# Keys and the retention's gate by seven products, head norms block by block, convolution taps moved behind

## The chip, the cores and the metric

One NeuronCore of a Trainium2 chip runs one two-layer block in fp32: a mixing stage, 32 routed experts, a second mixing stage, 16 routed experts. The metric is device microseconds of one execution, the median of several runs. Lower is better.

## The reference, cut to what matters

The change lies wholly in the first layer's mixing stage. There 256 latent tokens and 256 context tokens, each of 1024 numbers, go through the columns of one projection:

```python
u_ctx = h_ctx * (1 + csc) + csh
kv = u_ctx @ w_in[:, K_OFF:G_OFF] + b_in[K_OFF:G_OFF]
s_f = final_state(k_c, v_c, lg_f); s_b = final_state(k_c[:, ::-1], v_c[:, ::-1], lg_b)
u_lat = h_lat * (1 + sc) + sh
q, k, v, g, glu, gates = split(u_lat @ w_in + b_in)
q, k = rope(q), rope(k)
o = retention_bidir(q, k, v, lg_f, lg_b, s_f, s_b)       # 8 heads, keys of 128, values of 256
ret = silu(g) * head_norm(o)                             # 2048 columns
y_a = ret @ w_ret_out
z = za * sigmoid(zb)                                     # from glu
z = silu(layernorm(depthwise_conv(z, 31 taps))) 
y_b = z @ w_conv_out + b_conv_out
mix = (sigmoid(ga) * y_a + sigmoid(gb) * y_b) @ w_mix_out + b_mix_out
```

Keys (1024 columns) and values (2048) are wanted for latent and context tokens; queries, the gate g (2048), glu and gates for latent tokens alone.

## The kernel before

All engines run one hand-written order; they meet at semaphores. SyncE (SP) loads weights in blocks of 2 MB (1024 x 512 numbers) into eight bays of SBUF; in the mixing stage three of them (`ring`) take turns. `make_jobs` (line 84 on) lists the jobs and gives each load its bay, from `EARLY_BAYS` and then from `ROUNDS["mix1"]`; `load` (L404) issues a load when the last job that read its bay is done. So the place of a job in TensorE's order says when a later load can start.

TensorE's order in this stage: the modulation, glu, keys, queries, values, the heads, the gate g, the gates, then the output of the retention and of the convolution, and the mixing projection. A job of kind `cm8` is 32 matmuls of 128 x 128 by 256 columns (L835); a job of the gate g, kind `tm8`, is 16 matmuls of 512 columns (L846). The two key blocks have a job for latent (`cm8`) and one for context tokens (`cm8c`). The profile shows each fp32 matmul as two records.

The four value blocks are computed for latent and context tokens together by seven products instead of eight (Strassen's scheme over halves of the contraction and halves of the columns): `seven_products` (L942, matmuls at L957) multiplies sums of tokens (`u_sums`, made at L1453) by quarters of the weights or their sums (`add_weights`, L1455 to L1462). Each product is eight matmuls of 256 columns in one of four PSUM buffers `MB`. VectorE adds every product to the places it belongs to (`add_product`, L1482; two halves for products 0 to 4, one for 5 and 6; L1493, L1494, L1497), makes the next block's weight sums, and puts two taps of the convolution behind each product (`convolve`, L1400; taps at L1406 and L1408).

The convolution has 248 taps on VectorE, 8 channel tiles of 31. They are spread as filling over the stage: 64 during glu, 64 during the keys, 56 during the values, 16 in the heads, 48 during the gate g. Behind the last one comes the sum over channels (L1413), for which TensorE's `mean_of_sums` (L1026) waits after the last gates job.

The heads. TensorE per head h (L962 to L990): scores of head h+1 (two matmuls against the context keys, two against the latent ones), one of eight modulation jobs (L823), the output of head h. VectorE per head: the latent and the context scores times their decays (L1524, L1526), the argument of the decays of head h+2 (`decay`, L1475, L1476), statistics of head h-1 (L1513, L1516), the sum of two context decays of head h+2 (`context_decay`, L1481), two taps. ScalarE: copy of the output of head h-1 (L612), exponential of the decays of head h+2 (L596), four exponentials of the context decays (L606). The ties between them:

```python
pe.wait_ge(pc_sb, h)            # scores(h): VectorE's product with the context scores of head h-1
act.wait_ge(dec_arg, h + 1)     # decays(h): VectorE's decay(h)
act.wait_ge(pc_sb, h - 1)       # context_decays(h)
dve.wait_ge(eq_ready, h + 1)    # context_decay(h): ScalarE's exponentials
```

After the heads VectorE takes a copy of the last modulation, TensorE turns it (`turn_late`), VectorE folds it with gains and biases (`late_modulation`, L1355), normalises all 16 head tiles (L1548), and then per block of g adds the bias (L1440), waits for ScalarE's silu (L637) and multiplies (L1554). TensorE transposes the result (`turn_ret`, L1001) one block later.

Of the kernel before, what the change touches and what calls it, by code (L numbers as in the profile page):

```python
# [26 lines left out]
ALU = mybir.AluOpType  # L27
# [3 lines left out]
P = 128  # L31
D = 1024
L = 256
DT = D // P
# [41 lines left out]
ROUNDS = {"mix1": (2, 0, 1), "moe0": (4, 2, 3, 6, 5, 0, 1, 7), "mix2": (0, 1, 2, 4), "moe1": (7, 0, 3, 6, 1, 2, 4, 5)}  # L76
# [3 lines left out]
EARLY_BAYS = (0, 1, 0, 1, 2, 4, 5, 3, 0, 1, 2, 0, 1, 2, 1, 2, 1)  # L80
SUM_BAY = 0
# [5 lines left out]
def make_jobs():  # L87
# [11 lines left out]
    def experts(n):  # L99
        for e in range(EXPERTS[n] - 2):  # L100
            for q in range(3):
# [3 lines left out]
    order = (("mix1", (("ada", 4, ["ada"]), ("piece", PIECES, []), ("glu", 4, ["cm8"]), ("k", 2, ["cm8", "cm8c"]),  # L105
# [28 lines left out]
def build(nc, a):  # L134
# [3 lines left out]
    with ExitStack() as ctx:  # L138
# [105 lines left out]
        w_sums = [ring[:, SUM_BAY, D * i:D * (i + 1)].rearrange("p (a n) -> p a n", a=4) for i in range(4)] + [raw]  # L244
        retT, gT, mT, SQ = Vc, V, kT, qT
# [119 lines left out]
        def seven_wait(eng, b, p):  # L365

            if p == 6:
                eng.wait_ge(job_done, J["v", b, 0]["i"] + 1)
            else:
                eng.wait_ge(seventh, 6 * b + p + 1)  # L370

        def quarters(b):

            W = bays[loads[J["v", b, 0]["w"]]["bay"]].rearrange("p (k n) -> p k n", n=512)
            return W[:, 0:4, 0:256], W[:, 0:4, 256:512], W[:, 4:8, 0:256], W[:, 4:8, 256:512]
        lat1, lat2, ctx1, ctx2 = uT[:, 0:4, :], uT[:, 4:8, :], ucT[:, 0:4, :], ucT[:, 4:8, :]
# [122 lines left out]
        def _(pool):  # L499
# [5 lines left out]
            for n in range(8):  # L505

                if n >= 6:
# [29 lines left out]
        def _(act):  # L537
# [49 lines left out]
            for r, (src, b, bias) in enumerate((("k", 0, "b_k"), ("k", 1, "b_k"), ("q", 0, "b_q"), ("q", 1, "b_q"))):  # L587
                raw_copy(r, src, b, bias)
# [45 lines left out]
            for b in range(4):  # L634
                j = J["g", b, 0]
# [176 lines left out]
        def _(pe):  # L812
# [122 lines left out]
            for b in range(2):  # L935
                job(J["k", b, 0])
                pe.wait_ge(u_ready, PIECES + 1)
                job(J["k", b, 1])
# [1180 lines left out]
```

## Time and profile before

| | |
|---|---|
| median of 3 runs | 1500.07 us (1499.38 to 1500.78) |
| the profiled execution | 1499.55 us |
| its span | 1497.7 us |
| TensorE busy, over the span | 97% |
| VectorE, ScalarE busy | 36%, 15% |
| HBM read | 431.61 MB, 290 GB/s over the span |

The span is cut into instructions; a group names line, engine, operation and the tiles written and read. Idle time in front of a group is put down to what released it. A row of the timeline shows a run of like instructions: start, length, count. TensorE's rows overlap by the end of a matmul, some 0.16 us, so durations are best read from one start to the next. Of the mixing stage, TensorE spends 81 to 136 us on the keys, 136 to 164 on the queries, to 267 on the values, to 327 on the heads, to 385 on the gate g and to 441 on the gates.

### The profile page before, as it was taken

The numbers are of one execution on the slowest core, as the hardware profiler recorded it, in microseconds if no ns is written. First come the engines' busy times: TensorE is split into PE (matmuls) and PEld (weight loads), VectorE is DVE, ScalarE is ACT, GpSimd is POOL, SyncE is SP. The second block draws the span as 40 slices with busy tenths as digits, with TensorE's granted clock in tenths as the row PEclk, the third lists the DMA queues.
The fourth block names the chain that finished last, engine by engine and source line by source line (L and its number), as shares of the span: only waits on it lengthen the run. The fifth ranks groups of instructions, "written<-read, shape, count | busy, mean of one in ns | idle before, by whom it ended". The sixth has DMA issues, their size and how long they took to land.

```text
span 1497.7 us, 19676 instructions
## 1 busy us (share of the span) xinstructions
PE 1446.1 (97%) x8450; PEld 973.3 (65%) x8450; DVE 541.3 (36%) x1127; ACT 227.7 (15%) x438; POOL 17.8 (1%) x38
## 2 busy tenths in 40 slices
PE   8999899999999999999999998999999999999996
PEld 6888788664788887555544444445788886455542
DVE  0467898665402145222222111114223242211122
ACT  0210200321121004110111101012121022111011
POOL 0000000000000010000000000000010000000000
PEclk9999999999999999999999999999999999999999
DMA  9722132864343577999999999997564747999986
GB/s 382 294 97 93 57 113 78 310 258 162 133 168 131 225 313 278 369 426 427 428 426 426 427 429 427 427 417 314 151 223 156 286 169 303 429 428 427 427 339 257
DMA packets 36330, 435.43 MB, mean 291 GB/s; under 512 B 4353, under 2 KB 5769, under 8 KB 10009
## 3 DMA queue, kind: packets, MB, share of 16 engines
q1 hardware_dynamic: 33408, 427.89, 70.1%
q0 software_dynamic: 1664, 4.52, 1.0%
q10 hardware_dynamic: 1176, 1.84, 0.8%
q8 instruction: 64, 1.05, 0.3%
q14 instruction: 18, 0.14, 0.0%
HBM read 431.61 MB, written 2.62 MB: 290 GB/s over the span
## 4 chain that ended last, share of the span: by engine, by line
PE 80%; DMA 15%; DVE 4%; issue 0%; ACT 0%; SPq 0%; POOL 0%; DVEq 0%; POOLq 0%; ACTq 0%
PE PP L835 22%; PE PP L1146 17%; PE PP L1161 9%; PE MB L957 6%; PE MB L1130 5%; PE PP L846 5%; DMA ZC<-in_w_moe 5%; PE PP L873 3%; DMA RA<-in_w_moe 2%; DMA ring<-in_w_moe 2%; DMA Vc<-in_w_moe 2%; DMA uT<-in_w_moe 2%; PE PP L905 2%; PE PP L1122 1%; DMA ring<-in_w_ada 1%; DVE ZC L1408 1%
## 5 line engine op out<-in xcount | busy, mean ns | idle before, releaser
L835 PE MATMUL PP<-uT,ring 128*128 128x256 f32 x832 | 181.2, 379 | 0.0
L835 PEld LDWEIGHTS PP<-uT,ring 128*128 128x128 f32 x832 | 157.7, 190 | 21.8 <-issue 0.5
L1408 DVE SCALAR_TENSOR_TENSOR ZC<-ZC,vec 128x256 f32<-128x256 f32 x240 | 116.3, 484 | 7.9
L1815 DVE TENSOR_SCALAR V<-V 128x1 f32<-128x1 f32 x50 | 7.7, 154 | 307.2 <-PE PP L1146 307.2
L1146 PE MATMUL PP<-ring,const 128*64 128x256 f32 x992 | 112.1, 380 | 5.1 <-DMA ring<-in_w_moe 4.5
L1130 PE MATMUL MB<-V 64*128 64x512 f32 x400 | 112.4, 640 | 1.7 <-DVE V L1838 0.9
L1146 PEld LDWEIGHTS PP<-ring,const 128*64 128x64 f32 x992 | 72.2, 137 | 49.1 <-issue 11.6
L1830 DVE SCALAR_TENSOR_TENSOR V<-V 128x256 f32<-128x256 f32 x100 | 48.5, 485 | 108.7 <-PE MB L1130 94.0
L699 ACT ACTIVATE V<-PP 128x256 f32<-128x256 f32 x50 | 19.2, 385 | 380.1 <-PE PP L1146 380.1
L1161 PE MATMUL PP<-ring,const 128*64 128x512 f32 x336 | 76.7, 599 | 0.0
L846 PE MATMUL PP<-ring,uT 128*128 128x512 f32 x160 | 69.5, 593 | 0.0
L1146 PE MATMUL PP<-ZC,const 128*64 128x256 f32 x512 | 58.3, 380 | 7.7 <-DMA ZC<-in_w_moe 7.7
L1146 PE MATMUL PP<-RA,const 128*64 128x256 f32 x512 | 58.3, 380 | 3.9 <-DMA RA<-in_w_moe 3.7
L703 ACT ACTIVATE const<-small 128x512 f32 x50 | 31.8, 636 | 166.2 <-PE PP L1146 165.8
L1146 PEld LDWEIGHTS PP<-ZC,const 128*64 128x64 f32 x512 | 36.7, 137 | 30.1 <-DMA ZC<-in_w_moe 8.3
L835 PE MATMUL PP<-Vc,ring 128*128 128x256 f32 x256 | 55.6, 379 | 0.0
L1146 PEld LDWEIGHTS PP<-RA,const 128*64 128x64 f32 x512 | 36.6, 137 | 28.3 <-DMA RA<-in_w_moe 8.2
L846 PEld LDWEIGHTS PP<-ring,uT 128*128 128x128 f32 x160 | 30.1, 190 | 37.0 <-issue 37.0
L835 PEld LDWEIGHTS PP<-Vc,ring 128*128 128x128 f32 x256 | 48.6, 190 | 6.6
L1161 PEld LDWEIGHTS PP<-ring,const 128*64 128x64 f32 x336 | 22.3, 136 | 46.8 <-issue 45.1
L1836 DVE TENSOR_TENSOR V<-PP,uT 128x512 f32<-128x512 f32 x32 | 22.1, 692 | 80.4 <-PE PP L1161 80.4
L1130 PEld LDWEIGHTS MB<-V 64*128 64x128 f32 x400 | 30.3, 184 | 30.4 <-issue 30.2
(433 smaller groups left out, 1880.0 us busy)
## 6 DMA issues: line engine op xcount, KB each, us to landing
ring<-in_w_moe SPq DMA_DIRECT2D x54, 2048.0 KB, 18.9
RA<-in_w_moe SPq DMA_DIRECT2D x22, 2048.0 KB, 16.3
ZC<-in_w_moe SPq DMA_DIRECT2D x22, 2048.0 KB, 17.8
KQ<-in_w_moe SPq DMA_DIRECT2D x18, 2048.0 KB, 19.0
Vc<-in_w_moe SPq DMA_DIRECT2D x17, 2048.0 KB, 18.9
extra<-in_w_moe SPq DMA_DIRECT2D x17, 1792.0 KB, 16.5
ring<-in_w_ada SPq DMA_DIRECT2D x12, 2048.0 KB, 9.0
ring<-in_w_gates SPq DMA_DIRECT2D x7, 2048.0 KB, 8.0
```

What stands on the lines that cost most here:

```text
L703: nc.scalar.activation(xs, xsc[:, :, bass.ds(at, SLOTS)], ACT.Copy).then_inc(m["xs_ready"], 1)
L835: ins = pe.matmul(out[:, c, :], W[:, k * width + at:k * width + at + P], X[:, k, :], start=k == 0, stop=k == K - 1)
L846: ins = pe.matmul(out[:, 2 * t:2 * t + 2, :].rearrange("p a n -> p (a n)"), X[:, k, t * P:(t + 1) * P], W[:, k * 512:(k + 1) * 512], start ...
L873: ins = pe.matmul(out[:, c, :], W[:, k * 512 + c * P:k * 512 + (c + 1) * P], X[:, k, :], start=k == 0 and c % 2 == 0, stop=k == DT - 1 and ...
L905: ins = pe.matmul(glu_at(b, c), W[:, at:at + P], uT[:, k, :], start=k == 0 and c % 2 == 0, stop=k == DT - 1 and c % 2 == 1)
L957: ins = pe.matmul(MB[n % 4][:, t, :], x[:, k, t * P:(t + 1) * P], y[:, k, :], start=k == 0, stop=k == 3)
L1130: ins = pe.matmul(acc[t][g], S[rows, t * P:(t + 1) * P], ys[rows, :], start=first, stop=done == "acc_done", tile_position=(SLOTS * g, 0))
L1146: ins = pe.matmul(bank[q][SLOTS * g:SLOTS * (g + 1), 0:L], x[:, k, :], weights(W, k * 512 + g * 256, 256), start=k == 0, stop=k == DT - 1, ...
L1161: ins = pe.matmul(bank[2][SLOTS * g:SLOTS * (g + 1), :], hts[:, c % 2, SLOTS * (c // 2):SLOTS * (c // 2 + 1)], weights(W, c * D + g * 512, ...
L1408: ins = V_.scalar_tensor_tensor(conv[:, t, :], zpad[:, t, k:k + L], tap, conv[:, t, :], ALU.mult, ALU.add)
L1830: linked(V_.scalar_tensor_tensor(Sk[:, c], placer[:, c], slotcol, weightr[:, c], ALU.is_equal, ALU.mult), k, c + 2)
L1836: ins = V_.tensor_tensor(ys, bank[2], gate_row, ALU.mult)
```

## The change

- The keys get the seven products too. The order becomes queries, then six blocks of seven products (two of keys, four of values). For keys the weight sums stand as the stationary operand, so that the result has channels on partitions. Their weight sums go to the tiles of the values (`k_sums`). The rotations of queries come first; those of keys work in place once a block is complete.
- The gate g, wanted for latent tokens alone, gets seven products over halves of the latent's tokens, of the contraction and of the columns. A product there is four matmuls of 256 columns. VectorE makes five sums of half tokens (in head 1), five weight sums per block (those of the first block in heads 5, 6 and 7), adds every product to quarters of the block and works the bias in.
- The head norms are made for one block at a time, inside the gate blocks. The gate product of a block stands two products into the next one.
- Taps: 8 instead of 16 at each glu block, none beside the keys as such, 1, 1, 2, 2, 2, 4 behind a product in the six blocks (none where a rotation stands), 6 instead of 2 per head, and the 88 that are left after the last gate block. The folds of the modulation come behind them.
- Bays are renamed: the sums of weights use bay 2 instead of 0.

The diff, cut to its core:

```diff
-EARLY_BAYS = (0, 1, 0, 1, 2, 4, 5, 3, 0, 1, 2, 0, 1, 2, 1, 2, 1)
-SUM_BAY = 0
+EARLY_BAYS = (0, 1, 0, 1, 2, 4, 5, 3, 0, 1, 2, 0, 1, 0, 1, 0, 1)
+SUM_BAY = 2
...
-    order = (("mix1", (("ada", 4, ["ada"]), ("piece", PIECES, []), ("glu", 4, ["cm8"]), ("k", 2, ["cm8", "cm8c"]),
-                       ("q", 2, ["cm8"]), ("v", 4, ["seven"]), ("ada", 8, ["ada"]), ("g", 4, ["tm8"]), ("gates", 4, ["cm8"]),
+    order = (("mix1", (("ada", 4, ["ada"]), ("piece", PIECES, []), ("glu", 4, ["cm8"]), ("q", 2, ["cm8"]),
+                       ("k", 2, ["seven"]), ("v", 4, ["seven"]), ("ada", 8, ["ada"]), ("g", 4, ["seven"]), ("gates", 4, ["cm8"]),
...
-                    dense += (src != "ada" or b == 11) and (src, b) != ("glu", 2) and src != "v"
+                    dense += (src != "ada" or b == 11) and (src, b) != ("glu", 2) and src not in ("k", "v", "g")
...
+        k_sums = [home[:, 4 * i:4 * i + 4, :] for home in (V, Vc) for i in range(4)]
...
+        SEVEN = [("k", b) for b in range(2)] + [("v", b) for b in range(4)] + [("g", b) for b in range(4)]
+        G7 = 6
+        gate_raw = [small[:, i, :].rearrange("p (a n) -> p a n", a=LT) for i in range(2)]
+        halves = [[uT[:, 4 * k:4 * k + 4, P * t:P * (t + 1)] for k in range(2)] for t in range(LT)]
+        tok_sums = [extra[:, 512 * q:512 * (q + 1)].rearrange("p (a n) -> p a n", a=4) for q in range(5)]
+        of_half = lambda t, half: flat(t)[:, half * 2048:half * 2048 + 1024].rearrange("p (a n) -> p a n", a=4)
+        of_rest = lambda t, half: flat(t)[:, half * 2048 + 1024:(half + 1) * 2048].rearrange("p (a n) -> p a n", a=4)
+        g_sums = [[kw, of_half(V, 0), of_half(V, 1), Kc[:, 0:4, :], Kc[:, 4:8, :]],
+                  [of_rest(V, 0), of_rest(V, 1), KQ[:, 0:4, :], KQ[:, 4:8, :], KQ[:, 8:12, :]]]
...
+        def sum_at(i, q):
+
+            if i >= G7:
+                return g_sums[(i - G7) % 2][q]
+            return w_sums[q] if i >= 2 else k_sums[(5 * i + q) % 8]
+
+        def gate_bank(n):
+
+            x = J["gates", 0, 0]["pair"]
+            return PP[x if n % 4 < 2 else 1 - x][:, 2 * (n % 2), :]
         lat1, lat2, ctx1, ctx2 = uT[:, 0:4, :], uT[:, 4:8, :], ucT[:, 0:4, :], ucT[:, 4:8, :]
...
-                    j = J["g", n - 6, 0]
-                    pool.wait_ge(pair_free[j["pair"]], j["use"] + 1)
-                elif n >= 2:
-                    pool.wait_ge(seven_kept, 7 * (n - 1))
+                if n >= 2:
+                    pool.wait_ge(seven_kept, 7 * (n + 1))
...
+            for b in range(2):
+                act.wait_ge(seven_kept, 7 * (b + 1))
+                act.wait_ge(rope_done, 2 + b)
+                keys = kT[:, 4 * b:4 * b + 4, :]
+                nc.scalar.activation(swapped[0:64], keys[64:128], ACT.Copy)
...
+            for i in range(G7):
+                seven_products(i)
+
+            def gate_products(b):
+
+                i = G7 + b
+                B11, _, _, B22 = quarters(i)
+                made = 5 * G7 + 10 + 5 * b
+                for p, (x, y, sums) in enumerate(((tok_sums[0], B11, 5 * G7 + 6), (tok_sums[1], B22, 5 * G7 + 7),
+                                                  (halves[0][0], sum_at(i, 0), made + 1), (halves[1][1], sum_at(i, 1), made + 2),
+                                                  (tok_sums[2], sum_at(i, 2), made + 3), (tok_sums[3], sum_at(i, 3), made + 4),
+                                                  (tok_sums[4], sum_at(i, 4), made + 5))):
+                    n = 7 * i + p
+                    if p == 0:
+                        w_wait(pe, seven_job(i)["w"])
+                    pe.wait_ge(sums_made, sums)
+                    if n >= 7 * G7 + 4:
+                        pe.wait_ge(seven_kept, n - 3)
+                    elif n % 2 == 0:
+                        j = J["gates", p // 2, 0]
+                        pe.wait_ge(pair_free[j["pair"]], j["use"])
+                    for k in range(4):
+                        ins = pe.matmul(gate_bank(7 * b + p), x[:, k, :], y[:, k, :], start=k == 0, stop=k == 3)
+                    ins.then_inc(job_done if p == 6 else seventh, 1)
...
-                    j = J["k", 1, 1]
-                    pe.wait_ge(pair_free[j["pair"]], j["use"] + 1)
-                    pe.wait_ge(seven_kept, 26)
+                    pe.wait_ge(seven_kept, 40)
...
-                job(J["g", b, 0])
+                gate_products(b)
                 if b:
                     turn_ret(b - 1)
+            pe.wait_ge(seven_kept, 7 * len(SEVEN) - 2)
             job(J["gates", 0, 0])
             turn_ret(3)
+            pe.wait_ge(seven_kept, 7 * len(SEVEN))
             for b in range(1, 4):
...
+            def late_folds():
+
...
-                convolve(b * A_JOB, (b + 1) * A_JOB)
+                convolve(8 * b, 8 * (b + 1))
...
+            def add_weights(i, q):
+
+                if q == 0:
+                    w_wait(dve, seven_job(i)["w"])
+                if i == 1 and q >= 3:
+                    dve.wait_ge(seventh, q)
+                B11, B12, B21, B22 = quarters(i)
                 x, y, op = ((B12, B22, ALU.subtract), (B21, B11, ALU.subtract), (B11, B22, ALU.add), (B11, B12, ALU.add),
-                            (B21, B22, ALU.add))[i]
-                V_.tensor_tensor(w_sums[i], x, y, op).then_inc(sums_made, 1)
-            job_wait(dve, J["q", 0, 0])
-            for i in range(4):
-                add_weights(0, i)
-            rope(2)
-            rope(3)
-            add_weights(0, 4)
...
+            def taps(n):
+                tap_at[0] += n
+                convolve(tap_at[0] - n, tap_at[0])
+            tap_at = [step]
+            for i in range(G7):
                 for p in range(7):
-                    add_product(b, p)
-                    if p > 1 and b < 3:
-                        add_weights(b + 1, p - 2)
-                    convolve(step, step + 2)
-                    step += 2
-                if b < 2:
+                    add_product(i, p)
+                    if p > 1 and i + 1 < G7:
+                        add_weights(i + 1, p - 2)
+                    if (i, p) in ((0, 3), (1, 3), (2, 3)):
+                        rope(i + 1)
+                    else:
+                        taps((1, 1, 2, 2, 2, 4)[i])
+                if i in (2, 3):
...
-                convolve(step, step + 2)
-                step += 2
+                if h == 1:
+                    (a11, a12), (a21, a22) = halves
+                    for out, x, y, op in zip(tok_sums, (a21, a11, a11, a21, a12), (a22, a12, a22, a11, a22),
+                                             (ALU.add, ALU.add, ALU.add, ALU.subtract, ALU.subtract)):
+                        V_.tensor_tensor(out, x, y, op).then_inc(sums_made, 1)
+                if h == 5:
+                    add_weights(G7, 0)
+                elif h == 6:
+                    add_weights(G7, 1)
+                    add_weights(G7, 2)
+                elif h == 7:
+                    add_weights(G7, 3)
+                    add_weights(G7, 4)
+                taps(6)
...
+            def normalise(b):
+
+                for h in (2 * b, 2 * b + 1):
+                    for t in range(LT):
+                        o = On[:, t, h * DV:(h + 1) * DV]
+                        ins = V_.tensor_scalar(o, o, mv[:, t, h, 0:1], rstd[:, t * HEADS + h:t * HEADS + h + 1], ALU.subtract, ALU.mult)
+                link(ins)
+
+            def gate_ret(b):
+
                 dve.wait_ge(g_silu, b + 1)
                 o = On[:, :, b * 512:(b + 1) * 512]
-                say(dve, V_.tensor_tensor(o, o, raw2, ALU.mult), ret_ready, b + 1)
-                convolve(step + 12 * b, step + 12 * (b + 1))
...
+                one, two = ([out[:, t, 256 * half:256 * (half + 1)] for half in range(2)] for t in range(LT))
+                bias = [biasr[:, b % 2, 256 * half:256 * (half + 1)] for half in range(2)]
+                if p < 2:
+                    dve.wait_ge(bias_full[b % 2], 16 * ((4 + b) // 2 + 1))
+                    plus, minus = ((two[0], bias[0]), (two[1], bias[1])) if p == 0 else ((one[1], bias[1]), (one[0], bias[0]))
+                    V_.tensor_tensor(plus[0], M, plus[1], ALU.add)
+                    ins = V_.scalar_tensor_tensor(minus[0], M, -1.0, minus[1], ALU.mult, ALU.add)
+                else:
+                    for out in ((one[1], two[1]), (two[0], one[0]), (one[0], two[1]), (two[1],), (one[0],))[p - 2]:
+                        ins = V_.tensor_tensor(out, out, M, ALU.add)
+                say(dve, ins, seven_kept, n + 1)
+            for b in range(4):
+                for p in range(7):
+                    add_gate_product(b, p)
+                    if p == 1 and b:
+                        gate_ret(b - 1)
+                    if p > 1 and b < 3:
+                        add_weights(G7 + b + 1, p - 2)
+                    if p == 3:
+                        normalise(b)
+            gate_ret(3)
+            taps(DT * TAPS - tap_at[0])
+            late_folds()
 
```

## Rows read from the trace of the kernel before

**Rows 1.** Page, chain that ended last: share of the span by engine

```profile
PE 80%; DMA 15%; DVE 4%; issue 0%; ACT 0%; SPq 0%; POOL 0%; DVEq 0%; POOLq 0%; ACTq 0%
```

**Rows 2.** Chain in order of time, experts' stage: start us, us, what

```profile
836.53 34.22 DMA Vc<-in_w_moe
```

**Rows 3.** Timeline of TensorE, values: start us, us, engine, line, out<-in, records

```profile
108.67 13.98 PE L835 MATMUL PP<-uT,ring 128*128 128x256 f32 x64
...
163.93 7.07 PE L957 MATMUL MB<-ring,small 128*128 128x256 f32 x32
...
182.06 8.83 PE L957 MATMUL MB<-ring,extra 128*128 128x256 f32 x32 [4.16 <-DVE Vc L1494]
190.73 3.62 PE L957 MATMUL MB<-small,extra 128*128 128x256 f32 x16
...
266.70 1.03 PE L974 MATMUL MB<-KQ,Kc 128*128 128x256 f32 x4
```

**Rows 4.** Windows: us, busy of PE, PEld, DVE, ACT, POOL; PEclk, DMA share, GB/s

```profile
184.00:186.00 2.00, 2.00 (x6) 1.60 (x5) 1.89 (x5) 0.00 (x0) 0.00 (x0) 0.50 0.03 8
...
268.00:270.00 2.00, 0.59 (x3) 0.19 (x1) 1.93 (x5) 0.00 (x0) 0.49 (x1) 1.00 0.68 197
```

**Rows 5.** Timeline of TensorE, one head

```profile
284.71 1.03 PE L974 MATMUL MB<-KQ,Kc 128*128 128x256 f32 x4
...
286.53 1.92 PE L823 MATMUL PP<-ring,sT 128*32 128x512 f32 x16
...
291.94 1.03 PE L974 MATMUL MB<-KQ,Kc 128*128 128x256 f32 x4
```

**Rows 6.** Timeline of VectorE, the same head

```profile
282.89 0.69 DVE L1524 SCALAR_TENSOR_TENSOR small<-MB,small 128x512 f32<-128x512 f32 x1
...
284.09 0.74 DVE L1475 SCALAR_TENSOR_TENSOR small<-const,lgs 128x512 f32<-128x512 f32 x1
...
285.66 0.75 DVE L1513 BATCH_NORM_STATS2 bst<-RA 128x6 f32<-128x256 f32 x2
286.45 0.25 DVE L1516 BATCH_NORM_AGGREGATE mv<-bst 128x2 f32<-128x6 f32 x2
288.36 0.69 DVE L1481 TENSOR_TENSOR small<-small 128x512 f32<-128x512 f32 x1 [1.66 <-ACT small L606]
288.97 1.00 DVE L1408 SCALAR_TENSOR_TENSOR ZC<-ZC,vec 128x256 f32<-128x256 f32 x2
290.00 0.69 DVE L1524 SCALAR_TENSOR_TENSOR small<-MB,small 128x512 f32<-128x512 f32 x1
```

**Rows 7.** Timeline of ScalarE, the same head

```profile
285.66 0.63 ACT L596 ACTIVATE small<-small 128x512 f32<-128x512 f32 x1 [0.15 <-DVE small L1476]
286.19 2.06 ACT L606 ACTIVATE small<-const,wctx,lgs 128x256 f32<-128x256 f32 x4
```

**Rows 8.** Groups of VectorE by form: xcount, busy us, mean ns, idle before

```profile
L1462 DVE TENSOR_TENSOR ring<-ring 128x1024 f32<-128x1024 f32 x16 | 19.3, 1224 | 0.4
...
L1817 DVE TENSOR_TENSOR const<-PP,V 128x256 f32<-128x256 f32 x50 | 21.3, 426 | 2.3
```

**Rows 9.** SP's issue of the gate weights; DMA issues with median us to landing

```profile
310.21 13.07 SPq L415 DMA_DIRECT2D ring<-in_w_g  x3
...
ring<-in_w_g SPq DMA_DIRECT2D x4, 2048.0 KB, 8.2
```

**Rows 10.** Timeline of TensorE, the gate g: first job, first turn, first gates job

```profile
327.18 27.71 PE L846 MATMUL PP<-ring,uT 128*128 128x512 f32 x64
354.73 1.04 PE L1007 MATMUL MB<-const,RA 128*128 128x128 f32 x8
...
384.82 13.98 PE L835 MATMUL PP<-uT,ring 128*128 128x256 f32 x64
```

**Rows 11.** Timeline of VectorE, end of the convolution

```profile
394.14 3.68 DVE L1413 TENSOR_REDUCE rs<-ZC 128x256 f32<-128x2048 f32 x1
441.66 2.35 DVE L1562 TENSOR_TENSOR ZC<-ZC,MB 128x1024 f32<-128x1024 f32 x2 [43.84 <-PE MB L1029]
```

More of the change, by code:

```diff
@@ L586, in raw_copy @@
                 nc.scalar.activation(swapped[64:128], raw[0:64], ACT.Copy).then_inc(sig_ready, 1)
-            for r, (src, b, bias) in enumerate((("k", 0, "b_k"), ("k", 1, "b_k"), ("q", 0, "b_q"), ("q", 1, "b_q"))):
-                raw_copy(r, src, b, bias)
+            for b in range(2):
+                raw_copy(b, "q", b, "b_q")
+            for b in range(2):
+                act.wait_ge(seven_kept, 7 * (b + 1))
+                act.wait_ge(rope_done, 2 + b)
+                keys = kT[:, 4 * b:4 * b + 4, :]
+                nc.scalar.activation(swapped[0:64], keys[64:128], ACT.Copy)
+                nc.scalar.activation(swapped[64:128], keys[0:64], ACT.Copy).then_inc(sig_ready, 1)
             nfb = cst("nfb", 512)
@@ L933, in _, with seven_products @@
             pe.wait_ge(ld_rest, 32)
[L935 to L938, printed above, removed]
             job(J["q", 0, 0])
             job(J["q", 1, 0])
[L942 to L949 removed]
+            pe.wait_ge(u_ready, PIECES + 1)
+            def seven_products(i):
+                B11, _, _, B22 = quarters(i)
+                made = len(u_sums) + 5 * i
+                for p, (x, q, y, sums) in enumerate(((u_sums[0], None, B11, 1), (u_sums[1], None, B22, 2), (lat1, 0, None, made + 1),
+                                                     (ctx2, 1, None, made + 2), (u_sums[2], 2, None, made + 3),
+                                                     (u_sums[3], 3, None, made + 4), (u_sums[4], 4, None, made + 5))):
+                    n = 7 * i + p
                     if p == 0:
[L951 removed]
+                        w_wait(pe, seven_job(i)["w"])
                     pe.wait_ge(sums_made, sums)
@@ L1481, in context_decay, with add_product @@
                 V_.tensor_tensor(Eqd[:, q:q + 2, :], Eqd[:, q:q + 2, :], Eqb[:, q:q + 2, :], ALU.add)
-            def add_product(b, p):
-                n = 7 * b + p
-                seven_wait(dve, b, p)
-                M = MB[n % 4][:, :, :]
-                at = lambda i: slice(512 * b + 256 * i, 512 * b + 256 * (i + 1))
-                lat, ctx = [Vt[:, :, at(i)] for i in range(2)], [Vct[:, :, at(i)] for i in range(2)]
-                bias = [biasr[:, b % 2, 256 * i:256 * (i + 1)].unsqueeze(1).to_broadcast([P, LT, 256]) for i in range(2)]
+            def add_product(i, p):
+                n, (src, b) = 7 * i + p, SEVEN[i]
+                seven_wait(dve, i, p)
+                M = MB[(n + 2) % 4][:, :, :]
+                if src == "k":
+                    at = lambda half: slice(4 * b + 2 * half, 4 * b + 2 * half + 2)
+                    lat, ctx = [kT[:, at(half), :] for half in range(2)], [Kc[:, at(half), :] for half in range(2)]
+                    bias = [vec[:, VCOLS["b_k"] + 4 * b + 2 * half:VCOLS["b_k"] + 4 * b + 2 * half + 2].unsqueeze(2).to_broadcast([P, LT, L])
+                            for half in range(2)]
+                else:
+                    at = lambda half: slice(512 * b + 256 * half, 512 * b + 256 * (half + 1))
+                    lat, ctx = [Vt[:, :, at(half)] for half in range(2)], [Vct[:, :, at(half)] for half in range(2)]
+                    bias = [biasr[:, b % 2, 256 * half:256 * (half + 1)].unsqueeze(1).to_broadcast([P, LT, 256]) for half in range(2)]
                 if p < 2:
-                    dve.wait_ge(bias_full[b % 2], 16 * (b // 2 + 1))
+                    if src == "v":
+                        dve.wait_ge(bias_full[b % 2], 16 * (b // 2 + 1))
                     plus, minus = ((ctx[0], bias[0]), (ctx[1], bias[1])) if p == 0 else ((lat[1], bias[1]), (lat[0], bias[0]))
```

82 lines of the change are left out of this document (36 added, 46 removed).

## The prediction, made blind

> **What bounds the kernel now.** I read the page's chain of waits first [rows 1]: TensorE carries 80% of the chain that ended last, DMA 15%, VectorE 4%. Then the chain in order of time. Its DMA pieces lie in the experts' stage, where landings of 2 MB succeed each other [rows 2]; those loads are released by TensorE's jobs of the mixing stage, so whatever moves the end of the gate jobs moves them, and everything behind, by the same amount. The question is therefore only when TensorE finishes the last gate job and the mean of the convolution behind it.
>
> TensorE's timeline from the keys to the heads [rows 3] gives the unit of the sum. Each program matmul of 256 columns stands as two records; a job of 32 of them takes 13.98 us with its last end, 13.82 to the start of the next, so one costs 0.432 us, and a product of eight 3.455 us. The 28 products of the values would take 96.7 us; they take 266.70 - 163.93 = 102.8. The missing 6.0 us are one place: TensorE waits 4.16 us for VectorE ahead of 182.06, and the next 32 records take 8.67 us (182.06 to 190.73) in place of 6.91, 1.76 us more. The windows say why [rows 4]: at 184 to 186 us the granted clock was 0.50, the 1.2 GHz level, after a pause of 4.2 us. At 268 to 270 us, with TensorE idle for 1.58 us, it stayed at 1.00.
>
> The third reading decides. In the retention's head loop TensorE's period is 7.23 us (284.71 to 291.94, [rows 5]) and looks like the bound. But VectorE's period is 7.11 us (282.89 to 290.00, [rows 6]), and no wait in it is on TensorE: its one wait, 1.66 us, is for ScalarE's exponentials. These start when VectorE's own decay operations end: exponential of the decays at 285.66, four of the context at 286.19, done at 288.25 [rows 7], and VectorE goes on at 288.36. So VectorE's loop is a closed chain of its own work and ScalarE's, 0.12 us from setting the pace, and TensorE's scores of the next head wait for VectorE's second product of this one.
>
> **The change, part by part.**
>
> *Keys, and the stall of the values.* Two blocks of 64 matmuls (lat and ctx) become two of 56: 16 x 0.432 = -6.9 us. The sums of tokens and of the first weights now come while the two query jobs run, and the first two blocks carry one tap per product. VectorE per block: five updates of two halves at 1.32 us (0.61 + 0.71 from one start to the next, where one takes 0.69 busy), two of one at 0.72, five weight sums at 1.14 (1.22 busy [rows 8], 0.08 overlapped) = 13.8 us; with six taps and a rotation (three operations of 1024, 3.8 us) 20.7 us, against 24.2 us of TensorE. The third block has twelve taps, a rotation and two decays, 26.9 us, but enters with some 7 us of lead and 3 free product buffers. No block stalls TensorE, and the 6.0 us go too. The next weights land in time: a bay frees at a block's end and three products, 10.4 us, pass before VectorE asks for it, against a landing of 8.2 us [rows 9]. Sum: -12.9 us; heads start at 253.8 instead of 266.7. ScalarE's two swaps of key halves are released by the block's last update and are asked for three products later: nothing.
>
> *Head loop, taps.* Two taps per head become six. The wait for ScalarE doesn't shrink: it hangs on the decays, which stand ahead of it, while the taps stand behind it. A tap costs 0.52 (two in 1.03, 288.97 to 290.00, [rows 6]), so the period becomes 7.11 + 4 x 0.52 = 9.2 us, above TensorE's 7.23. VectorE now sets the pace, and TensorE pauses 2.0 us before each scores.
>
> *Head loop, sums of half tokens.* In head 1 five additions of 512 elements, five times 0.61 = 3.05 us, in the same chain: +3.05.
>
> *Head loop, weights of the first gate block.* In head 5 VectorE waits for that block's weights. Its bay is freed by the modulation job of head 5; before, the load was issued at 310.21, the moment that job ended, and took 8.2 us [rows 9]. The job ends 3.8 us after the second product of head 5 (0.15 to TensorE, 1.8 scores, 1.9 job, [rows 5]); with issue and landing the weights are there 12.2 us after it. VectorE reaches the wait after decays 1.57, statistics 1.06, the wait of 1.7 and the addition 0.6, 4.9 us. It stands 7.3 us, with the taps and the products of heads 6 and 7 queued behind it, and TensorE's scores of head 7 wait for those. Then five weight sums: 1.14 here, 2.28 in each of heads 6 and 7. Before, nothing of VectorE waited for these weights.
>
> *The stage laid end to end.* Last product 253.8; VectorE's last update and four taps behind it, first two score products: 258.1. Six periods of 9.2 (heads 0 to 5), 55.3; sums of tokens 3.05; head 5's wait and sum 8.5: second product of head 6 at 324.9. Head 6 without decays: 1.06 + 2.28 + 3.12 + 1.2 = 7.7: 332.6. Head 7: 0.7 wait for the copied output, 1.06, 2.28, 3.12: 339.8. The copy of the modulation, 512 elements, takes 0.7 and TensorE's four small products some 0.85: gate products start at 341.4. The stage takes 87.7 us where it took 327.18 - 266.70 = 60.5: +27.2 us.
>
> *Clock.* TensorE's pause in heads 5 and 6 is 10.5 us, longer than the one that cost 1.76 us. I take 1.75 once: the output of head 6 is on the path there, as its statistics hold VectorE. In head 2 (5.0 us pause) a loss of that size hides in the next pause of 2.0. Bounds 0 (hidden) and 3.5 (another in head 7).
>
> *Gate products.* 4 x 28 matmuls of 0.432 = 48.4 and three turns of 0.88 (1.04 with its overlap) give 51.0; before, 384.82 - 327.18 = 57.6 [rows 10]: -6.6 us. VectorE needs per block five updates of two quarters (0.81) and two of one (0.46), from the nearest row of that form, 0.426 busy [rows 8]; five weight sums 5.7; four head norms at 0.35, the start-to-start of that form, 1.4; one gate product 1.26: 13.3 us against 12.97. Four buffers carry this 0.3 us; if an update of two takes 0.96, the low end of the lead is lost and it costs 1.7. I take 0. ScalarE's silu of 1.1 us starts at a block's end and is asked for two products, 3.5 us, later. POOL's bias loads are released one block ahead of use, as before.
>
> *Behind.* 88 taps are left for after the last gate: 45.7 and the reduction 3.7 [rows 11], 49.4 us. TensorE has 56.1 us of gate jobs. VectorE ends 4.5 us ahead, the folds of 1.7 us (nine operations of under 0.25) fit as well; before it idled 43.8 us there, until the mean released it at 441.66. Cost 0, and this cover is nearly gone: VectorE is what would be late next.
>
> *Sum.* -12.9 + 27.2 + 1.75 - 6.6 = +9.4 us on the profiled execution's 1499.55 us (span 1497.7), 0.5 us under the median of 1500.07: **1509.0 us**.
>
> **Rules of the skill.** The Trainium skill ("TensorE: Matmul & The Clock Gate", "A second HAM failure mode: psum-queue depth-cycling") says that short idles between groups of matmuls, if frequent, make the clock swing between its levels. This would speak against a head loop with a pause of 2 us in every 9.2. The short pause of rows 4 does not show it; by the rule the time would be the last rival's.
>
> **Rivals.**
> *The stretched loop hides (faster).* If the six taps fitted into the 1.66 us wait and the gate weights were there, the head stage would keep its 60.5 us, and only -12.9 and -6.6 would remain: 1480. It decides at TensorE's waits ahead of scores: none means this. Against it: the order of operations [rows 6, 7] puts taps behind the wait, and the load cannot be issued before head 5's job. Chance 0.08.
> *Pace only.* If the wait for the gate weights were absent (an earlier landing), the weight sums alone would remain and the stage be 5 to 6 us shorter: 1503 without clock loss. For it: only that one load's timing; against: the 310.21 issue. Chance 0.10.
> *VectorE late behind (slower still).* If updates of quarters run at the high bound, the gate stage grows by 1.7 and the tail eats the 4.5 us: 1511 to 1514. Chance 0.10.
> *Clock down through the heads.* At 1.2 GHz throughout, a head is 14.5 us and sets the pace: 8 x 14.5 = 116 us in place of 89.4: 1535. Chance 0.04.
> *The change does less than it says.* The edits replace every key and gate matmul, so the 32 fewer program matmuls are certain; no chance is set on it.
>
> **How the numbers follow.** The forecast holds 0.68. About 0.2%, 3 us, is what a measurement of this kernel can tell from no change. Range 1503 to 1513: its low end is pace only, its high end the clock's high bound with the quarter updates'; the two far rivals (0.12) and some of the third stay outside. Faster 0.09; same 0.06, out of pace only with a gain elsewhere; slower 0.85.
>
> **What would show it.** Right: TensorE's values without a wait; scores 9.2 us apart for most heads, each released by VectorE's second product; one wait of VectorE of about 7 us on the load of the gate weights in head 5; scores of head 7 some 10 us late; gate stage 51 us; the mean of the sums about 448 to 451 us and the first expert loads later by the same. Wrong: a head period still at 7.2, no VectorE wait on that load, or a wait of TensorE for the sum of the convolution.

## The result, and the profile after

The changed kernel takes 1513.28 us in the median (1512.98 to 1515.43), the kernel before 1500.4 (four runs); the ratio is 1.0091, with a 95% interval of 1.0077 to 1.0106. It is slower, as forecast, but by 13 us where +9.4 us were forecast, and 0.3 us above the range. The profiled execution took 1513.3 us with a span of 1511.3, 13.6 us more than the 1497.7 of the profiled execution before.

| stage, by TensorE | before | after | difference | forecast |
|---|---|---|---|---|
| start of the heads | 266.70 | 253.45 | -13.25 | -12.9 |
| heads, to the first gate product | 60.48 | 89.66 | +29.18 | +28.95 (27.2 and 1.75 of clock) |
| gate g, to the first gates job | 57.64 | 52.66 | -4.98 | -6.6 |
| gates jobs, to the mean of the convolution | 56.14 | 56.13 | 0.0 | 0 |
| mean of the convolution, sum so far | 440.96 | 451.90 | +10.94 | +9.4 |
| second routing (the one ahead of the second experts) | 7.76 | 10.15 | +2.39 | not foreseen |

TensorE's waits for VectorE in the mixing stage, in the view of waits (us in total, times, longest), where before 4.2 us stood ahead of the values:

```profile
PE MB L1024 <- DVE small L1588: 20.4, 6, 10.0
...
PE PP L942 <- DVE small L1612: 2.3, 1, 2.3
```

None stands ahead of a product any more; six stand ahead of scores, all released by VectorE's second product of a head (L1588), 20.4 us together, one of them 10.0. TensorE's timeline of the stage, the answer to [rows 5, 10]:

```profile
253.45 1.03 PE L1024 MATMUL MB<-KQ,Kc 128*128 128x256 f32 x4
...
297.91 1.10 PE L1024 MATMUL MB<-KQ,Kc 128*128 128x256 f32 x4 [1.14 <-DVE small L1588]
...
307.10 1.10 PE L1024 MATMUL MB<-KQ,Kc 128*128 128x256 f32 x4 [1.72 <-DVE small L1588]
...
324.55 2.04 PE L1024 MATMUL MB<-KQ,Kc 128*128 128x256 f32 x4 [9.98 <-DVE small L1588]
...
342.12 1.14 PE L942 MATMUL PP<-const,small 128*128 128x8 f32 x8 [2.30 <-DVE small L1612]
343.11 5.30 PE L1011 MATMUL PP<-ring,extra 128*128 128x256 f32 x16
348.25 1.89 PE L1011 MATMUL PP<-small,uT 128*128 128x256 f32 x8
...
395.77 13.98 PE L863 MATMUL PP<-uT,ring 128*128 128x256 f32 x64
...
451.90 0.59 PE L1081 MATMUL MB<-rs,const 128*128 128x256 f32 x2
```

Heads 4 and 5 start 9.2 us apart (297.91, 307.10), head 7's scores 17.5 us after head 6's. The turn of the last modulation waits 2.3 us, and the first 16 records of the gate products (343.11 to 348.25) take 5.14 us in place of 3.45. VectorE's timeline of heads 4 and 5, the answer to [rows 6], and one row of head 7:

```profile
302.55 3.08 DVE L1463 SCALAR_TENSOR_TENSOR ZC<-ZC,vec 128x256 f32<-128x256 f32 x6
305.66 0.69 DVE L1586 SCALAR_TENSOR_TENSOR small<-MB,small 128x512 f32<-128x512 f32 x1
...
306.87 0.74 DVE L1523 SCALAR_TENSOR_TENSOR small<-const,lgs 128x512 f32<-128x512 f32 x1
...
308.43 0.75 DVE L1575 BATCH_NORM_STATS2 bst<-RA 128x6 f32<-128x256 f32 x2
...
311.13 0.69 DVE L1529 TENSOR_TENSOR small<-small 128x512 f32<-128x512 f32 x1 [1.66 <-ACT small L635]
318.85 1.23 DVE L1513 TENSOR_TENSOR small<-ring 128x1024 f32<-128x1024 f32 x1 [7.03 <-DMA ring<-in_w_g]
319.99 3.08 DVE L1463 SCALAR_TENSOR_TENSOR ZC<-ZC,vec 128x256 f32<-128x256 f32 x6
323.11 0.69 DVE L1586 SCALAR_TENSOR_TENSOR small<-MB,small 128x512 f32<-128x512 f32 x1
...
334.98 0.75 DVE L1575 BATCH_NORM_STATS2 bst<-RA 128x6 f32<-128x256 f32 x2 [2.92 <-ACT RA L641]
```

Six taps end head 4 (302.55 to 305.66); then two products, decays, statistics, the wait of 1.66 us for ScalarE and the addition at 311.13. Behind it stands the wait of the change: 7.03 us for the first gate block's weights, whose load SP issued at 310.98, when head 5's modulation job was done:

```profile
310.98 46.43 SPq L441 DMA_DIRECT2D ring<-in_w_g  x4
```

It is ended 7.9 us later, at 318.85. In head 7 VectorE waits another 2.92 us, for ScalarE's copy of the output of head 6, which TensorE computes behind its pause of 10.0 us. The end of the convolution, the answer to [rows 11]:

```profile
443.73 3.68 DVE L1468 TENSOR_REDUCE rs<-ZC 128x256 f32<-128x2048 f32 x1
...
452.61 2.35 DVE L1667 TENSOR_TENSOR ZC<-ZC,MB 128x1024 f32<-128x1024 f32 x2 [3.63 <-PE MB L1081]
```

VectorE's reduction ends at 447.4; the mean leaves TensorE without a wait, at 451.90, and VectorE idles 3.6 us where it idled 43.8. The granted clock in the pause ahead of head 7 and over the first gate products (columns as in [rows 4]):

```profile
320.00:325.00 5.00, 0.45 (x1) 0.48 (x2) 4.79 (x11) 0.00 (x0) 0.00 (x0) 0.50 0.00 0
...
343.00:344.00 1.00, 1.00 (x4) 0.91 (x4) 0.52 (x4) 0.18 (x1) 0.00 (x0) 0.50 0.04 16
...
345.00:346.00 1.00, 1.00 (x4) 0.82 (x3) 0.00 (x0) 0.34 (x1) 0.00 (x0) 0.50 0.00 0
```

From 320 us to 324.55 TensorE stands, and the clock is at its lower level (0.50, 1.2 GHz); it is still there when the scores of head 7 start. It is at that level again from 343 to 346 us, over the first gate products.

### The profile page after: what moved, and what is told of

It is laid out like the page before. It is cut to its first block, busy times and chain, and to the rows that moved or that the text cites. A ratio compares the mean times of both kernels' runs of the same rounds, so it can differ in the third digit from the quotient of the medians.

```text
span 1511.3 us, 19959 instructions
## 1 busy us (share of the span) xinstructions
PE 1442.9 (95%) x8514; PEld 991.1 (66%) x8514; DVE 605.8 (40%) x1228; ACT 224.4 (15%) x430; POOL 17.8 (1%) x38
## 4 chain that ended last, share of the span: by engine, by line
PE 79%; DMA 15%; DVE 4%; ACT 1%; issue 0%; SPq 0%; POOL 0%; DVEq 0%; POOLq 0%
PE PP L863 20%; PE PP L1198 17%; PE PP L1213 9%; PE MB L987 6%; PE MB L1182 5%; DMA ZC<-in_w_moe 5%; PE PP L1011 3%; PE MB L985 3%; PE PP L901 3%; DMA RA<-in_w_moe 2%; DMA Vc<-in_w_moe 2%; DMA ring<-in_w_moe 2%; DMA uT<-in_w_moe 2%; PE PP L933 2%; PE PP L1174 1%; DVE ZC L1463 1%
## 5 line engine op out<-in xcount | busy, mean ns | idle before, releaser
L863 PE MATMUL PP<-uT,ring 128*128 128x256 f32 x704 | 153.2, 379 | 0.0
L863 PEld LDWEIGHTS PP<-uT,ring 128*128 128x128 f32 x704 | 133.4, 190 | 18.5 <-issue 0.5
L1198 PE MATMUL PP<-KQ,const 128*64 128x256 f32 x384 | 43.7, 380 | 1.4 <-DMA KQ<-in_w_moe 1.1
L901 PE MATMUL PP<-KQ,ring 128*128 128x256 f32 x192 | 42.2, 379 | 0.3 <-DVE KQ L1999 0.3
```

The lines of the kernel that those rows point to most:

```text
L863: ins = pe.matmul(out[:, c, :], W[:, k * width + at:k * width + at + P], X[:, k, :], start=k == 0, stop=k == K - 1)
L901: ins = pe.matmul(out[:, c, :], W[:, k * 512 + c * P:k * 512 + (c + 1) * P], X[:, k, :], start=k == 0 and c % 2 == 0, stop=k == DT - 1 and ...
L1198: ins = pe.matmul(bank[q][SLOTS * g:SLOTS * (g + 1), 0:L], x[:, k, :], weights(W, k * 512 + g * 256, 256), start=k == 0, stop=k == DT - 1, ...
```

## The experiments

**Sums behind the heads.**

```diff
-                if h == 5:
-                    add_weights(G7, 0)
...
                 taps(6)
+            for q in range(5):
+                add_weights(G7, q)
```

> The changed kernel with the five weight sums of the first gate block behind the last head instead of in heads 5, 6 and 7; the six taps per head stay. Theory of the prediction (VectorE's wait for the gate weights in head 5 is in series with the heads): that wait of 7.0 us and the 10.0 us pause of TensorE ahead of the scores of head 7 go, five sums of 1.14 us come behind the heads, so the gate products start at about 336 to 338 us instead of 343.1, the heads still 9.2 us apart, and the time is 1505 to 1509 us. Rival (the wait is only moved, the heads hide it): VectorE waits as long for something else and the time stays within 1 us of 1513.3.

Measured: 1506.77 us, ratio to before 1.0035 (1.0023 to 1.0048), 6.5 us under the changed kernel (the kernel before took 1501.42 in this series, 1.0 more than beside the changed one). TensorE's waits in the stage:

```profile
PE MB L1024 <- DVE small L1588: 11.9, 5, 4.7
PE PP L942 <- DVE small L1606: 5.7, 1, 5.7
```

The wait of 10.0 us ahead of head 7 is gone (the longest is 4.7, in head 1 with its token sums); one of 5.7 us, for VectorE's sums behind the last head, stands in its place. The gate products start at 337.20 in place of 343.11. So the load wait was in series with the heads. The 5.9 us are net and not the price of that wait alone: the fall of the clock behind the 10.0 us pause is gone too, while VectorE now waits 2.9 us for the output of head 6 with nothing to do meanwhile, and the turn behind the 5.7 us takes 1.7 us at the lower clock in place of 1.0. The second routing fell to the lower clock here too.

**Two taps per head.**

```diff
-                taps(6)
+                taps(2)
```

> The changed kernel with two taps per head instead of six, the 32 others behind the last gate block. Theory: the heads go back to 7.2 us apart (9.2 in the changed kernel), the 7 us wait for the gate weights stays, the gate products start at about 327 to 330 us, but 120 taps are left behind the last gate block, 62 us of VectorE with the reduction 66, against 56 us of TensorE, so that TensorE waits some 10 to 12 us for the sum of the convolution; time 1507 to 1511. Rival (the heads are paced by something else, such as ScalarE's copies): period stays near 9 us and the time rises above 1518 by the later tail.

Measured: 1512.09 us, ratio 1.0075 (1.0058 to 1.0092), 1 us above what was expected. TensorE's scores and first gate product, and its waits:

```profile
291.04 1.03 PE L1024 MATMUL MB<-KQ,Kc 128*128 128x256 f32 x4
...
298.27 1.03 PE L1024 MATMUL MB<-KQ,Kc 128*128 128x256 f32 x4
...
313.49 2.04 PE L1024 MATMUL MB<-KQ,Kc 128*128 128x256 f32 x4 [7.83 <-DVE small L1588]
...
329.10 1.11 PE L1011 MATMUL PP<-ring,extra 128*128 128x256 f32 x4
```

```profile
PE MB L1024 <- DVE small L1588: 12.5, 3, 7.8
PE MB L1081 <- DVE rs L1468: 12.0, 1, 12.0
```

Heads go back to 7.23 us (291.04 to 298.27), so it was the taps that set the pace. The load wait stays (7.8 us ahead of head 7's scores, which come 15.2 us after head 6's, 298.27 to 313.49), and the gate products start at 329.10, 14.0 us earlier than in the changed kernel. Nearly all of it is given back at one place: TensorE waits 12.0 us for the sum of the convolution (L1468). Here TensorE pauses only 0.3 us ahead of the turn, and the first 16 records of the gate products take 3.5 us: the 1.7 us lost there in the changed kernel do not occur. So six taps per head were wrong by where they stood, and fewer alone is no cure: the work has to go somewhere where VectorE idles.

**VectorE's work laid where it idles.**

```diff
             rope(0)
+            taps(16)
...
-                        taps((1, 1, 2, 2, 2, 4)[i])
+                        taps((3, 3, 1, 2, 2, 4)[i])
...
-                if h == 5:
+                if h == 6:
                     add_weights(G7, 0)
-                elif h == 6:
-                    add_weights(G7, 1)
-                    add_weights(G7, 2)
                 elif h == 7:
-                    add_weights(G7, 3)
-                    add_weights(G7, 4)
-                taps(6)
+                    for q in range(1, 5):
+                        add_weights(G7, q)
+                taps(2 if h != 1 else 0)
```

> The changed kernel with VectorE's work laid where it idles: 16 taps ahead of the first product, 3 instead of 1 per product in the two key blocks, 1 instead of 2 in the third, 2 per head (0 in head 1), the gate weights asked for in head 6 (one sum) and head 7 (four). Theory: no wait of TensorE in the products, heads 7.2 us apart but for head 1 and the load, gate products start at 316 to 322 us, mean of the convolution at 427 to 431 us against 441.0 before; time 1486 to 1491, faster than both. Rival (the seven-product gate costs more than its 51 us, or the clock falls at each pause): above 1495.

> The tuned kernel again, beside the others on the same chip: span 1485 to 1488, the time 1488 to 1491 us as in its first run; the yardstick for keys_only and tuned_filled.

Measured: 1490.69 us, ratio 0.9936 (0.9920 to 0.9953), and in the second series 1490.16 us, 0.9927 (0.9910 to 0.9944): faster than both kernels, 23 us under the changed one with the same work. Its TensorE in the first series' profile, late heads and then the mean:

```profile
295.08 1.03 PE L1024 MATMUL MB<-KQ,Kc 128*128 128x256 f32 x4
...
302.31 1.03 PE L1024 MATMUL MB<-KQ,Kc 128*128 128x256 f32 x4
...
318.52 1.06 PE L942 MATMUL PP<-const,small 128*128 128x8 f32 x8 [3.31 <-DVE small L1609]
319.44 5.39 PE L1011 MATMUL PP<-ring,extra 128*128 128x256 f32 x16
```

```profile
428.31 0.59 PE L1081 MATMUL MB<-rs,const 128*128 128x256 f32 x2
```

These heads are 7.23 us apart, VectorE's wait for the gate weights is down to 3.6 us, and the mean comes at 428.31, inside the 427 to 431 laid out. The first gate products lose 1.8 us here too (319.44 to 324.66).

**The keys' part alone.**

```diff
-                       ("k", 2, ["seven"]), ("v", 4, ["seven"]), ("ada", 8, ["ada"]), ("g", 4, ["seven"]),
+                       ("k", 2, ["seven"]), ("v", 4, ["seven"]), ("ada", 8, ["ada"]), ("g", 4, ["tm8"]),
...
-                gate_products(b)
+                job(J["g", b, 0])
...
+                with_bias(J["g", b, 0], 4 + b, raw2)
+                dve.wait_ge(g_silu, b + 1)
...
+                taps(15)
```

> The keys by seven products and the order of the changed kernel (queries first, 16 taps ahead of the first product, 3, 3, 1, 2, 2, 4 per product, 2 per head), but the gate g as before: 16 matmuls of 512 columns per block, all head norms ahead, 15 taps per gate block. Theory (the keys' part brings its 12.9 us whole, and only the gate's part loads the head loop): heads 7.2 us apart, gate g of 57.6 us, mean of the convolution at 427 to 430 us, span near 1485, the time 1486 to 1490 us: the same within 2 us as the tuned kernel that has the seven-product gate too, since that one gives the gate's 6.6 us back in the heads. Rival (the gate's part is worth its 6.6 us in the tuned kernel): this one is slower than tuned by 5 us or more.

Measured: 1491.54 us, ratio 0.9935 (0.9919 to 0.9952), 1.5 us above what was expected, against 1490.16 of the tuned kernel beside it: 1.4 us, less than either's interval. TensorE's first gate job, first gates job and mean:

```profile
316.88 27.71 PE L878 MATMUL PP<-ring,uT 128*128 128x512 f32 x64
...
374.52 13.98 PE L867 MATMUL PP<-uT,ring 128*128 128x256 f32 x64
...
430.65 0.59 PE L1083 MATMUL MB<-rs,const 128*128 128x256 f32 x2
```

The gate g takes its 57.6 us again (316.88 to 374.52), the heads 63.2 us (they began at 253.66). In the first profile of the tuned kernel the heads take 66.8 us (252.60 to 319.44) and the gate g 52.7 (from there to the first gates job, which starts 56.1 us ahead of the mean at 428.31); in its second they take 68.9 and 53.0. So the gate's seven products save 4.6 to 4.9 us in their own stage and cost 3.6 to 5.7 in the heads, where their token sums, their weight sums and the wait for a load stand. From the first scores to the mean it is 177.0 us with the keys' part alone, 175.7 and 178.0 with both: whether the gate's part is worth anything is not shown. The keys' part, with its order and its taps, has the gain over the kernel before without it.

**TensorE kept busy in its pauses.**

```diff
+            def fill(n):
+                spare = PP[J["gates", 0, 0]["pair"]]
+                for _ in range(n):
+                    pe.matmul(spare[:, 3, 0:P], ident, ones, start=True, stop=True)
...
                 if h:
+                    fill({1: 10, 3: 20, 7: 44}.get(h, 6))
                     pe.wait_ge(p_sb, h)
...
             def turn_late():
+                fill(9)
```

> The changed kernel with idle matmuls of 128 columns on TensorE ahead of its waits in the heads (10, 20 and 44 ahead of the scores of heads 1, 3 and 7, 6 ahead of the others, 9 ahead of the turn behind the last head), so that it doesn't stand still there. Theory (two falls of the clock are on the path: behind the 10 us pause and at the first gate product, 1.75 us each): granted clock 1.00 from 250 to 350 us, gate products start at 341 to 342 us and the gate stage takes 51 us, the mean at about 448.5 in place of 451.9, time 1509 to 1511 us. Rival (the losses are hidden by VectorE's pace): the time stays within 1 us of 1513.3.

Measured: 1507.86 us, ratio 1.0046 (1.0030 to 1.0063), 5.4 us under the changed kernel and 1.1 us below what was expected. The granted clock over the whole stage (columns as in [rows 4]):

```profile
250.00:300.00 50.00, 48.26 (x293) 37.20 (x292) 40.04 (x79) 12.77 (x24) 0.54 (x1) 1.00 0.67 249
300.00:350.00 50.00, 49.08 (x312) 38.60 (x311) 34.36 (x72) 10.36 (x17) 0.00 (x0) 1.00 0.48 178
```

It stays at 1.00 in both. From the first scores to the mean TensorE takes 194.3 us (255.48 to 449.80) where the changed kernel takes 198.45: -4.1 us. Where they come from is in VectorE's row of head 7 and TensorE's of the first gate products, to set beside those of the changed kernel:

```profile
334.57 0.75 DVE L1583 BATCH_NORM_STATS2 bst<-RA 128x6 f32<-128x256 f32 x2 [0.62 <-ACT RA L641]
```

```profile
342.62 3.70 PE L1012 MATMUL PP<-ring,extra 128*128 128x256 f32 x16
346.15 1.89 PE L1012 MATMUL PP<-small,uT 128*128 128x256 f32 x8
```

VectorE waits 0.62 us for the output of head 6 in place of 2.92, so the fall in head 7 had cost 2.3 us and not the 1.75 of my theory; the first 16 records take 3.53 us in place of 5.14, another 1.6. The profiled execution began its heads 2.0 us later by a fall at 20 us, far from the edit, so its absolute times stand that much too high; its second routing ran at full clock (7.8 us). Why the median is 5.4 us lower and the stage 4.1 is not settled; in the profiled execution the second routing gives 2.4 and the start takes 2.0.

The tuned kernel with idle matmuls in its own pauses:

```diff
+                    fill({1: 10, 3: 5}.get(h, 0))
...
+                fill(14)
```

> The tuned kernel with idle matmuls on TensorE in its pauses (10 ahead of the scores of head 1, 5 of head 3, 14 ahead of the turn behind the last head). Theory: the clock stays up at the first gate product, where tuned lost 1.75 us (5.2 us for the first 16 records in place of 3.45), mean at 426.5 to 427 in place of 428.3, time 1.5 to 2 us under tuned. Rival (the loss there is not from the pause of 3.3 us): same as tuned within 0.5 us.

Measured: 1488.86 us, ratio 0.9923 (0.9904 to 0.9942), 1.3 us under the tuned kernel beside it, inside their scatter and between theory and rival. From the first scores to the mean the trace has 173.9 us (255.23 to 429.17) against 175.7 (252.60 to 428.31) in the tuned kernel's first profile and 178.0 in its second, so -1.8 and -4.1 us; the first 16 records of the gate products take 3.5 us (321.98 to 325.52) in place of 5.2 and 5.5. The theory of the loss at the first gate product holds.

**When the second routing comes.** The kernel before with extra matmuls in the first gates job:

```diff
+                        if (j["src"], j["b"], nth) == ("gates", 0, 0):
+                            for _ in range(25):
+                                pe.matmul(out[:, c, :], W[:, at:at + P], X[:, 0, :], start=True, stop=True)
```

> The kernel before with 25 extra matmuls of 256 columns (10.8 us) in the first gates job, so that all that follows comes 10.8 us later, as in the changed kernel, without any of its edits. Theory (the last 2.4 us of the changed kernel are TensorE's clock in the second routing, which depends on when it comes): the routing before the second experts runs partly at 1.2 GHz as in the changed kernel, span 1497.7 + 10.8 + 2.4 = 1510.9. Rival (they belong to the change's own edits): granted clock 1.00 there, span 1508.5.

> The kernel before with 8 extra matmuls (3.5 us) in the first gates job. Theory: everything behind moves rigidly by 3.5 us, whatever the loads of the experts do, span 1501.2, plus 2.4 if the second routing falls. Rival (the stage of the experts, bound by its loads, absorbs part): under 1500.

Measured, one execution each: 1510.14 us with a span of 1508.3 for 25 matmuls, and 1503.97 us, span 1502.2, for 8. The first is the rival's number: everything moved by 10.6 us and nothing was added. The second moved by 4.5 us, of which 3.5 are the matmuls; the fall behind the values' stall was longer there (its mean already came 4.0 us later). In both the experts' stage absorbed none of the delay. My theory, that the routing falls because it comes 10.8 us later, is not borne out by the first: it came as late and ran at full clock. One execution can't exclude that a later routing falls more often.

**The same kernels again.**

> The changed kernel once more, to see which of its clock losses return. Theory (the falls in the heads and at the first gate product follow from TensorE's pauses, the one in the second routing comes and goes): gate products start at 343 us within 2, their first 16 records take over 4.5 us, the second routing runs at either level; span 1509 to 1513. Rival (the fall in the second routing belongs to the change): it is there again at the same place, 2.4 us.

> The kernel before once more. Theory (the fall in the second routing comes and goes with the run): either level there; where it falls the span is 1500 and not 1497.7. Rival (it belongs to the change): granted clock 1.00 in the second routing and a span of 1497.7 to 1498.5.

Measured, one execution each: 1515.05 us, span 1513.0, and 1501.13 us, span 1499.3. In the changed kernel the gate products start at 343.68 and the fall in the second routing is there again (10.2 us); in the kernel before it is not (7.76 us), and its 1.6 us above the first profile are a fall at 20 us. By these four alone the fall would belong to the change. But the tuned kernel shows both. The windows of the second routing in the changed kernel, in the tuned kernel's first profile and in its second, two microseconds each:

```profile
1239.00:1241.00 2.00, 1.96 (x9) 1.96 (x10) 1.90 (x5) 0.00 (x0) 0.00 (x0) 0.50 0.58 238
```

```profile
1215.00:1217.00 2.00, 1.49 (x13) 1.49 (x14) 1.87 (x6) 0.00 (x0) 0.00 (x0) 1.00 0.73 303
```

```profile
1220.00:1222.00 2.00, 1.28 (x6) 1.29 (x7) 1.90 (x6) 0.00 (x0) 0.00 (x0) 0.50 0.93 385
```

The same instructions ran at 1.00 in one execution (routing of 7.77 us) and at 0.50 in the other (10.20). Of the profiles here, five show the fall (the changed kernel twice, sums behind, keys alone, tuned in its second) and the other eight don't. All five are of kernels with the keys' part (five of nine); the four profiles of the kernel before, two of them with extra matmuls, have none. So the tuned kernel shows that the fall comes and goes with the same instructions, but not that it comes without the change: whether the change makes it likelier is open. The time at which the routing comes does not decide it alone: the matmuls that ran slow begin at 1219.1 to 1239.7 us (keys alone, the changed kernel again), the same ones at full clock at 1215.5 to 1238.7 (tuned, two taps).

## Why the prediction was right and wrong

- *The bound.* Right: TensorE's end of the gate jobs moved, and the experts' stage passed the shift on, 10.94 us at the mean and 10.82 at the last loads of the first experts; the run with 25 matmuls shows it without the change.
- *Keys, and the stall of the values.* Right: -13.25 us for -12.9, no wait ahead of any product.
- *Taps in the head loop.* Right: 9.2 us a head, and 7.23 with two taps.
- *The wait for the gate weights.* Right: 7.03 us for 7.3, in head 5, 10.0 us of TensorE; that it is in series with the heads is shown by the run with the sums behind, 5.9 us net.
- *The stage end to end.* Right in sum, +29.2 us for +28.95, and in part by luck: with idle matmuls in the pauses, at full clock, the stage takes 87.14 us (255.48 to 342.62), +26.7 for the forecast's 27.2, and the falls in the heads take 2.5 for its 1.75. The two misses cancel.
- *Behind.* Right: 88 taps fit by 4.5 us, with 3.6 us idle left.
- **Clock** is the step that failed: one loss of 1.75 us in the whole sum, with a high bound of another in head 7, and the question only which long pause was on the path. The one loss in the heads measured 2.3 us (VectorE's wait of 2.92 us for the output of head 6 against 0.62 at full clock). The one in head 2, taken as hidden, is hidden but for 0.2 (a VectorE period of 9.42 us, 287.05 to 296.47, in place of 9.2). And a second fall stood on the path: the short wait ahead of the turn (2.3 us) and the turn itself were followed by a fall over the first gate products, 5.14 us for 16 records in place of 3.45, where every product is on the path. These 1.7 us are the miss of the "Gate products" term (-5.0 for -6.6), which I had priced at full clock. The idle matmuls give all of this back (-4.1 us), and in the run with two taps, without that short wait, the first products ran at full clock.
- The second 2.4 us, in the second routing, lie in a stage that I took as rigid. It has pauses of its own (1.42 and 1.27 us before, 1.42 and 0.90 after), and ran at full clock in the one execution that I read. One profile of the kernel before could not show that this varies. With 1.7 and 2.4 the forecast of 9.4 is 13.5, against 13.6 of the spans. That the clock fell there is shown; why is open. Whether the runs without a profile had the second one can't be seen.
- *The rivals.* Pace only, faster, and VectorE late behind are refuted by the waits of the changed kernel. "Clock down through the heads" held in part: the clock fell in three of the pauses but came back each time within a head, and with the fall at the gate it took 4.1 us, not 26. The Trainium skill ("TensorE: Matmul & The Clock Gate", "A second HAM failure mode: psum-queue depth-cycling") says that frequent short idles between groups of matmuls make the clock swing between its levels. The trace agrees only in part: the clock fell behind the pauses of 2.6, 4.7, 10.0 and 2.3 us, and not behind those of 0.2, 1.1 and 1.7 us ahead of other heads, which are the frequent short ones.

## What to carry to other kernels

A loop that looks bound by one engine can be 2% from being bound by a closed chain of two others: before putting filler work into it, add up that chain, including the wait that the filler doesn't shorten. Ask of every moved operation what it waits for and when that can be there at the earliest; here a load whose buffer another job holds, asked for one head too early, stopped two engines. And where a change makes TensorE pause, price the clock at each place where it starts again on the path, not once; idle matmuls in the pauses can buy it back (4.1 us here). A profile shows one execution: two of the same kernel differed by 8.8 us of span.

## What was not expected

The granted clock fell at a pause of 2.3 us with the four small products of the turn behind it (0.50 from 343 to 346 us, 1.7 us lost), although at 18.2 to 20.5 us of the kernel before's first profile a pause of the same length left it at 1.00. In its second profile the early pause (2.5 us) cost 1.7 us. The loss at such a short pause thus comes and goes between executions of one kernel. The tuned kernel shows it in head 1, first profile and second:

```profile
257.12 1.10 PE L1024 MATMUL MB<-KQ,Kc 128*128 128x256 f32 x4 [2.62 <-DVE small L1588]
```

```profile
259.82 1.99 PE L1024 MATMUL MB<-KQ,Kc 128*128 128x256 f32 x4 [2.62 <-DVE small L1588]
```

The tuned kernel's two profiled executions, of the same instructions, have spans of 1485.4 and 1494.2 us; of these 8.8 us the heads begin 2.7 late (252.60, 255.31), the mean comes another 2.3 late (428.31, 433.34), and 2.4 are the second routing; the rest I did not trace.
